# Row pitch and placement of the split activations, with a smaller software-DMA scratch

## The reference

```
x += 0.5 * SwiGLU_a(RMSNorm(x))      # D = 1024, FF = 2816
x += Mixer_l(RMSNorm(x))             # l = 0: retention || Mamba-2 SSD; l = 1: latent attention over paged cache
x += 0.5 * SwiGLU_b(RMSNorm(x))
...                                  # both layers, then a final RMSNorm

def swiglu(h, w_in, w_out):
    gate, up = jnp.split(h @ w_in, 2, axis=-1)
    return (jax.nn.silu(gate) * up) @ w_out
```

## Time and profile before

| | |
|---|---|
| median of 3 runs | 2287.21 us |
| profiled execution, its own time | 2294.08 us |
| its span | 2292.4 us |
| granted TensorE clock | 0.992 of 2.4 GHz |
| PE busy | 2248.4 us, 98% |
| weight loads (PEld) busy | 2167.7 us, 95% |
| DVE / ACT / POOL busy | 1115.0 / 812.2 / 171.2 us |
| chain that ended last | PE 90%, line L360 alone 82% |

### The profile page before, as it was taken

The page is one execution under the profiler, slowest core; times in us unless marked ns, Lnnn a source line. Parts: engine busy times, 40 slices in busy tenths (PEclk is TensorE's granted clock), DMA queues, the critical chain, the costliest instruction groups (busy, mean ns, idle before and its releaser), DMA issues.

```text
span 2292.4 us, 48657 instructions
## 1 busy us (share of the span) xinstructions
PE 2248.4 (98%) x19482; PEld 2167.7 (95%) x19482; DVE 1115.0 (49%) x1773; ACT 812.2 (35%) x1420; POOL 171.2 (7%) x243
## 2 busy tenths in 40 slices
PE   9999999999999999999999999999999989999998
PEld 9999999997888999999999999999986689999997
DVE  4444434786436544444344444434557745444433
ACT  4333333562324433333333333233346524333222
POOL 0000001022100010000010000001114501000000
PEclk9999999999999999999999999999999999999999
DMA  4333334233333232333332323333547723332333
GB/s 146 92 92 92 97 102 117 77 103 94 122 115 111 84 102 83 92 92 92 107 106 88 92 92 92 101 103 102 159 143 248 260 86 90 93 93 92 92 106 107
DMA packets 119872, 249.49 MB, mean 109 GB/s; under 512 B 15360, under 2 KB 15632, under 8 KB 118400
## 3 DMA queue, kind: packets, MB, share of 16 engines
q1 hardware_dynamic: 105552, 193.05, 28.3%
q0 software_dynamic: 14048, 54.49, 6.9%
q10 hardware_dynamic: 144, 0.09, 0.0%
HBM read 237.30 MB, written 9.95 MB: 108 GB/s over the span
## 4 chain that ended last, share of the span: by engine, by line
PE 90%; DVE 5%; ACT 2%; issue 1%; POOL 1%; DMA 0%; SPq 0%; DVEq 0%; ACTq 0%
PE psum L360 82%; PE psum L2358 1%; PE psum L2373 1%; PE psum L1165 1%; DVE w_low L338 1%; DVE conv_sum L1595 1%; PE psum L2445 1%; DVE probs_by_key L2785 0%; PE psum L2343 0%; PE psum L1152 0%; PE psum L2403 0%; PE psum L2325 0%; ACT probs L2518 0%; PE psum L1010 0%; PE psum L2299 0%
## 5 line engine op out<-in xcount | busy, mean ns | idle before, releaser
L338 DVE TENSOR_TENSOR w_low<-w_raw,w_high 128x512 fp32r<-128x512 f32 x718 | 510.2, 729 | 619.3 <-ACT w_high L332 618.5
L360 PE MATMUL psum<-x_high,w_high 128*128 128x260 f32 x3840 | 773.5, 283 | 6.4 <-DVE w_low L338 3.3
L360 PE MATMUL psum<-x_low,w_high 128*128 128x260 f32 x3840 | 770.3, 282 | 0.0
L360 PE MATMUL psum<-x_high,w_low 128*128 128x260 f32 x3840 | 769.0, 282 | 0.0
L360 PEld LDWEIGHTS psum<-x_high,w_high 128*128 128x128 f32 x3840 | 589.0, 188 | 13.0 <-DVE x_low L642 2.4
L332 ACT ACTIVATE w_high<-w_raw 128x512 fp32r<-128x512 f32 x718 | 433.8, 623 | 452.7 <-PE psum L360 439.5
L360 PEld LDWEIGHTS psum<-x_low,w_high 128*128 128x128 f32 x3840 | 591.7, 188 | 0.0
L360 PEld LDWEIGHTS psum<-x_high,w_low 128*128 128x128 f32 x3840 | 590.7, 188 | 0.0
L360 PE MATMUL psum<-hidden_high,w_low 128*128 128x260 f32 x1408 | 278.8, 279 | 0.0
L360 PE MATMUL psum<-hidden_high,w_high 128*128 128x260 f32 x1408 | 278.7, 279 | 0.0
L360 PE MATMUL psum<-hidden_low,w_high 128*128 128x260 f32 x1408 | 278.6, 280 | 0.0
(11 more groups left out here) (395 smaller groups left out, 1659.6 us busy)
## 6 DMA issues: line engine op xcount, KB each, us to landing
w_raw<-in_weights_dram SPq DMA_DIRECT2D x720, 256.0 KB, 2.7
cache_pages<-in_cache_pages_dram POOLq DMA_DIRECT2D x128, 272.0 KB, 4.2
ret_sample_state<-in_state_ret_dram POOLq DMA_DIRECT2D x2, 2048.0 KB, 8.3
out_ret_s_dram<-ret_sample_state POOLq DMA_DIRECT2D x2, 2048.0 KB, 6.6
out_y_dram<-residual SPq DMA_DIRECT2D x8, 260.0 KB, 2.2
ssm_sample_state<-in_state_ssm_dram POOLq DMA_DIRECT2D x2, 1024.0 KB, 5.8
out_ssm_s_dram<-ssm_sample_state POOLq DMA_DIRECT2D x2, 1024.0 KB, 4.8
residual<-in_x_dram SPq DMA_DIRECT2D x3, 520.0 KB, 6.7
```

Source lines behind the costliest of these rows:

```text
L338: nc.vector.tensor_tensor(WL[:, slot, :], WRAW[:, slot, :], WH[:, slot, :].bitcast(F32), ALU.subtract).then_inc(w_split, 1)
L360: mm = nc.tensor.matmul(PS[:, b0 + 2 * m + half, 0:cols], w, x[:, half * cols:(half + 1) * cols], start=start, stop=stop)
```

## The change

`x_high` and `x_low` get rows of 576 floats, 2304 bytes apart, of which the first 520 floats are used. The cursor is moved on by 128 bytes before them and by 128 bytes behind them. The scratch of the software DMAs shrinks from 16384 to 8192 bytes, and everything moves down with it.

The new addresses: `residual` starts at 8320. `x_high` starts at 25088 = 98*256, `x_low` at 43520 = 170*256, so all 16 rows stand at 0 modulo 256. `w_raw` starts at 62080, which is 128 modulo 256. From there on every tile lies 4352 = 17*256 bytes lower than before, so modulo 256 nothing else moves: the weight tiles and the hidden rows stand at 128. `keys` and `w_uk_by_head` go with `x_high` from 128 to 0. The instructions of all engines, their order and their waits are the same.

```diff
+SCRATCH = 8192
+ROW = 576
...
-    BASE = 16512
+    BASE = SCRATCH + 128
     cursor = [BASE]
...
     XT, _ = sb("residual", [P, KD, T])
-    XH, XH_OFF = sb("x_high", [P, KD, T], F32R)
-    XL, XL_OFF = sb("x_low", [P, KD, T], F32R)
+    cursor[0] += 128
+    XHR, XH_OFF = sb("x_high", [P, KD, ROW], F32R)
+    XLR, XL_OFF = sb("x_low", [P, KD, ROW], F32R)
+    XH, XL = XHR[:, :, 0:T], XLR[:, :, 0:T]
+    cursor[0] += 128
     WRAW, _ = sb("w_raw", [P, R, CW])
...
-    HROW = 576
     HH_OFF = (REGION + 127) // 256 * 256 + 128
-    HH = at("hidden_high", [P, KF, HROW], HH_OFF, F32R)[:, :, 0:T]
-    HL = at("hidden_low", [P, KF, HROW], HH_OFF + (KF * HROW * 4 + 255) // 256 * 256, F32R)[:, :, 0:T]
+    HH = at("hidden_high", [P, KF, ROW], HH_OFF, F32R)[:, :, 0:T]
+    HL = at("hidden_low", [P, KF, ROW], HH_OFF + (KF * ROW * 4 + 255) // 256 * 256, F32R)[:, :, 0:T]
...
-    nc = bacc.Bacc("TRN2", target_bir_lowering=False, num_devices=1)
+    nc = bacc.Bacc("TRN2", target_bir_lowering=False, num_devices=1, dynamic_dma_scratch_size=SCRATCH)
```

## The result

The changed kernel takes 2314.48 us (median of 4 runs, 2312.42 to 2315.60), the kernel before 2286.93 us (4 runs, 2286.52 to 2289.23). The ratio is 1.0116, with a 95% interval of 1.0102 to 1.0131: 1.2% slower. The forecast was 2294 us with a range of 2255 to 2304. The direction was right, the size was not, and the time lies outside the range.

The account below looks back on a forecast made before the run. The prediction took TensorE's matmul pace, which depends on where moving rows lie and what ran before, as the bound. It added 7 us for x rows and 0 for the rest to 2287.21, giving 2294 us, range 2255 to 2304.

Parts of the forecast that it names:

- The x rows' place: All 11,616 matmuls over x: pace from 119.07 to 119.7 ns at the new place, +7.3 us.
- row k=4: FFN input tile already at 0 modulo 256 before the change: 119.2 ns per matmul, its second half 120.0.
- the unquiet row k=0: First input tile in the mixer's output projection: 120.0 ns per matmul, straight after matmuls over rows at other places.
- No quiet pattern at distance 128: x rows at 0, weights at 128 modulo 256: forecast unquiet at 2294 us, 118.7 to 121.0 ns, chance 0.62.
- The hidden rows: Second FFN projection: must stay at 123.1 us for 1056 matmuls, since nothing of it moved modulo 256.
- Quiet everywhere: Rival for matmuls over x: uniform rows bring the quiet pattern, -29 us to 2258 us, chance 0.26.
- No difference: Rival for matmuls over x: the pace stays at 119.07 ns, 2287 us, chance 0.10.
- The scratch as a wait: Rival for cache page DMAs: the halved scratch makes POOL wait, up to 67 us, 2354 us, chance 0.02.
- The rule on weight loads: TensorE: loading next weights takes no read bandwidth, so placement would be free and the sum 0; weighed as the no-difference case.

Follow-up runs that it names:

- experiment 2: The changed kernel with its small scratch and new addresses, but x rows 2080 bytes apart from 128 modulo 256 as before: 2289.70 us, ratio to before 1.0001.
- experiment 4: The kernel before with hidden rows at 0 modulo 256 instead of 128, nothing else: 2304.59 us, ratio to before 1.0063.
- experiment 3: The changed kernel with four small extra matmuls ahead of the first hidden row of each FFN: 2307.19 us, ratio to before 1.0066.
- experiment 6: Three kernels: the changed kernel with x rows 32 below, 64 above or 32 bytes above the weights' place modulo 256: 2307.91, 2306.18 and 2290.09 us.
- experiment 1: The changed kernel without its two steps of 128 bytes, so x rows at 128 modulo 256 like weights and hidden rows: 2275.57 us, ratio to before 0.9939.
- experiment 5: The changed kernel with weight tiles, x rows and hidden rows all at 0 modulo 256: 2267.95 us, ratio to before 0.9924.
- experiment 7: Weights, x and hidden rows all at 0 modulo 256, plus four small extra matmuls ahead of each FFN's hidden rows, against the changed kernel: 2293.27 us.
- experiment 8: The changed kernel with weights, x and hidden rows all at 0 modulo 256, everything 256 or 512 bytes higher than in experiment 5: 2277.27 and 2278.71 us.

## Why the prediction was wrong

**The x rows' place: right in the mechanism.** The pace after was forecast as 119.7 ns from three readings and is 120.0. The stretch was to be 237.0 us and is 237.6. The four FFNs hold 7920 of the 11,616 x matmuls and lost 4 x 1.84 = 7.4 us. The same 0.93 ns for the 3696 of the mixers would be 3.4 us more, but their stages show less: 0.8 us in the first mixer against experiment 2, and nothing that can be told from the clock in the attention stage. So the term is 7.4 to 11 us against 7.3 forecast. The readings of row k=4 and of the unquiet row k=0 were the right ones to use. "No quiet pattern at distance 128" held in the changed kernel and in experiment 4.

**The hidden rows: the step that failed.** The prediction said of the second projection that it "must stay at 123.1 for 1056, since nothing of it moved modulo 256". It is 126.6, four times 3.5 us, 14 us in all. This term was put at nothing in the sum, and the range did not cover it: without it the kernel would have stood near 2300 us, inside the range. Experiments 2, 3 and 6 show what stands in its place. At distance 0 TensorE has two stable patterns, 116.7 and 120.0 ns, and what runs just before a stretch decides which of them the whole stretch gets. With the x rows of before the entry led to quiet in eight FFNs of eight (the kernel before and experiment 2); with x rows all at distance 128 it led to unquiet in four of four. That this holds for every execution is not shown, but all four runs of the changed kernel lie within 3.2 us.

The rest of the miss, some 5 us, is most likely the clock in the attention stage: the forecast started from runs of before of 2286.5 to 2289.2 us, 5 to 8 us below its profiled execution, which had that drop of the clock.

The argument for the hidden rows was at hand. The prediction itself read from the earlier trace rows that "what came before decides which one it falls into; the place alone does not", and then used this for x only. The change altered what comes before every hidden stretch. By that reading the quiet of the hidden rows could be an outcome of their entry too, and so at risk, at a price of 4 x 3.5 us on the slower side.

**The rivals.** Quiet everywhere was not what happened, but experiments 1 and 5 show it at distance 0, with x at the forecast 116.7 ns. No difference: fell. The scratch as a wait: fell, experiment 2 being equal to before within 0.1%.

**The rule on weight loads.** The Trainium skill, page "TensorE: Matmul & The Clock Gate", section "Step-by-step: what each phase is for", says that loading the next weights takes no read bandwidth from the running matmul. The prediction read from it that placement would be free. By these runs it is not: experiments 1 and 5 differ from the changed kernel in placement alone, and by 39 and 47 us in the medians. Whether the loads take bandwidth, or placement acts in another way, no run shows.

## What to carry to other kernels

Where weight loads and moving rows are read together at every matmul, as here, it is worth trying both at the same place modulo 256 bytes with a row pitch that is a multiple of 256: of the 20 x stretches at distance 0 in experiments 1, 5, 7 and 8, 17 were quiet, and the three that were not are all in a first FFN. Measure the matmul start intervals stretch by stretch. A stretch can lock into a fast or a slow pattern, so a change at one operand can make an untouched stretch behind it 3% slower; list what runs ahead of every stretch that depends on it. Compare such layouts over several runs, since one unlucky entry is worth 10 us here.

## What the runs showed of the hardware

- Matmul interval at 2.4 GHz with a 128x128 weight load for each 128x260 float32r product: 116.7 ns in the quiet pattern, 120.0 in the locked unquiet one, 119.1 where the rows' distance changes every 12 matmuls or is +32.
- The unquiet pattern at distance 0 repeats every four matmuls, with start intervals of about 118, 120, 118 and 124 ns; the quiet one has 115 to 118 ns throughout.
- Either pattern was reached within the first ten or so matmuls of a stretch and then lasted all of it, 1056 or 1980 matmuls, without a break. That the two read streams meet in SBUF is the natural reading, since only their distance mattered; by which mechanism they do was only argued, not shown.
- The unquiet pace of 120.0 ns was the same at uniform distances of -32, +64 and 128 and, after an unlucky entry, at 0; only +32 gave 119.1.
